# Two decoder blocks on one core: mixers of the first block in another order, and five borders between stages with other waits

## What is computed

```python
def first_block(x, ...):
    h = x
    for i in range(DEPTH):
        z = rms_norm(h, g_mix[i]) @ w_in[i]
        z_a, z_b, z_c = split_cols(z, (A_COLS, B_COLS, C_COLS))
        y_a = chunked_spatial_gating(z_a, ...)
        y_b = rwkv7_time_mix(z_b, ...)
        y_c = nsa_attention(z_c, ...)
        h = h + jnp.concatenate([y_a, y_b, y_c], axis=-1) @ w_out[i]
        hn = rms_norm(h, g_ffn[i])
        f = swiglu(hn, ...) if i % 2 == 0 else moe_swiglu(hn, router_w[j], router_b[j], ...)
        h = h + f
        gate = jax.nn.sigmoid(rms_norm(h, g_ple[i]) @ ple_gate_w[i])
        h = h + (p[i] @ ple_proj_w[i]) * gate
    return rms_norm(h, g_final)

def second_block(x, c, ...):
    for l in range(DEPTH):
        h = rmsnorm(x, norm_mix_g[l]) * (1.0 + sc1) + sh1
        ...
        x = x + g1 * (mix @ w_out[l])
        h = rmsnorm(x, norm_ffn_g[l]) * (1.0 + sc2) + sh2
        x = x + g2 * ((jax.nn.silu(h @ ffn_w1[l]) * (h @ ffn_w3[l])) @ ffn_w2[l])
    return rmsnorm(x, final_g)
```

## Time and profile before

| | |
|---|---|
| median of 3 runs | 2163.87 us (2160.41 to 2163.98) |
| the profiled execution | 2163.64 us, of which the span is 2162.3 us |
| busy share of the span | PE 97%, DVE 34%, ACT 18%, POOL 3% |
| mixers of layer 0 up to the start of its feed-forward part | to 212.4 us |
| the same mixers in layer 1 | 467.64 us later |
| mixture of experts | about 694 to 1396 us |
| borders mixb / ffnb of the second model | 1448 and 1806.6 / 1566 and 1924.7 us |

### The profile page before, as it was taken

The page is one execution under the profiler, slowest core; times in us unless marked ns, Lnnn a source line. Parts: engine busy times, 40 slices in busy tenths (PEclk is TensorE's granted clock), DMA queues, the critical chain, the costliest instruction groups (busy, mean ns, idle before and its releaser), DMA issues.

```text
span 2162.3 us, 28139 instructions
## 1 busy us (share of the span) xinstructions
PE 2092.4 (97%) x11815; PEld 1203.5 (56%) x11815; DVE 726.4 (34%) x1486; ACT 399.0 (18%) x896; POOL 60.7 (3%) x63
## 2 busy tenths in 40 slices
PE   8989999999978899999999999999999999999998
PEld 5665777765754333322333233366677775757775
DVE  2664376322773100000000000137546643831112
ACT  2344000032452000000101001153300002410001
POOL 0021000000110000000000000000000000000000
PEclk9999999999989999999999999999999999999999
DMA  6222985333222999999999999733677642474130
GB/s 233 90 109 87 424 348 219 113 123 117 87 122 102 406 426 416 417 425 413 425 414 425 425 424 425 287 139 122 257 307 267 239 182 83 133 321 144 61 127 20
DMA packets 61235, 535.26 MB, mean 248 GB/s; under 512 B 9200, under 2 KB 9712, under 8 KB 23120
## 3 DMA queue, kind: packets, MB, share of 16 engines
q1 hardware_dynamic: 49216, 474.30, 54.1%
q10 hardware_dynamic: 9216, 50.34, 6.4%
q0 software_dynamic: 2672, 8.78, 1.1%
HBM read 527.74 MB, written 7.75 MB: 248 GB/s over the span
## 4 chain that ended last, share of the span: by engine, by line
PE 85%; DVE 8%; DMA 4%; ACT 2%; issue 1%; POOL 0%; DVEq 0%; SPq 0%; ACTq 0%
PE ps L92 85%; DVE ring L92 5%; DMA ring<-in_moe 4%; DVE stat L92 1%; ACT ring L92 1%; DVE natural L92 0%; DVE gates L92 0%; DVE transposed L92 0%; POOL ring L92 0%; DVE residual L92 0%; ACT natural L92 0%; ACT L92 0%; DMA residual<-in_x 0%; ACT z L92 0%; DVE z L92 0%
## 5 line engine op out<-in xcount | busy, mean ns | idle before, releaser
L92 PE MATMUL ps<-ring 128*32 128x512 f32 (+10 forms) x3784 | 537.4, 521 | 22.0 <-DMA ring<-in_moe 8.4
L92 PE MATMUL ps<-ring,z 128*32 128x512 f32 (+3 forms) x2048 | 476.3, 584 | 5.3 <-ACT ring L92 4.5
L92 PE MATMUL ps<-ring,transposed 128*128 128x384 f32 (+4 forms) x1408 | 470.3, 490 | 3.1 <-DVE transposed L92 2.4
L92 PE MATMUL ps<-transposed,ring 128*128 128x257 f32 (+2 forms) x2128 | 470.4, 379 | 1.3 <-DVE transposed L92 1.3
L92 PEld LDWEIGHTS ps<-transposed,ring 128*128 128x128 f32 (+1 forms) x2128 | 400.2, 189 | 85.3 <-issue 30.4
L92 PEld LDWEIGHTS ps<-ring 128*32 128x32 f32 (+4 forms) x3784 | 200.0, 130 | 302.0 <-issue 279.4
L92 PEld LDWEIGHTS ps<-ring,transposed 128*128 128x128 f32 x1408 | 260.4, 191 | 185.2 <-issue 61.3
L92 PEld LDWEIGHTS ps<-ring,z 128*32 128x32 f32 (+2 forms) x2048 | 172.3, 139 | 254.3 <-issue 240.4
L92 DVE TENSOR_TENSOR z<-z,ps 128x256 f32<-128x256 f32 (+4 forms) x100 | 43.0, 430 | 627.7 <-ACT z L92 607.0
L92 ACT COPY z<-ps 128x256 f32<-128x256 f32 (+6 forms) x110 | 45.7, 415 | 507.7 <-PE ps L92 507.2
L92 ACT ACTIVATE z<-ps 128x256 f32<-128x256 f32 (+2 forms) x87 | 32.6, 374 | 421.8 <-PE ps L92 212.0
(11 more groups left out here) (154 smaller groups left out, 1011.5 us busy)
## 6 DMA issues: line engine op xcount, KB each, us to landing
ring<-in_moe SPq DMA_DIRECT2D x87, 2048.0 KB, 19.3
ring<-in_ffn SPq DMA_DIRECT2D x66, 1536.0 KB, 9.6
ring<-in_moe SPq DMA_DIRECT2D x90, 1024.0 KB, 17.8
ring<-in_w_in SPq DMA_DIRECT2D x25, 1536.0 KB, 6.6
z<-in_ada ACTq DMA_DIRECT2D x48, 768.0 KB, 5.3
ring<-in_w_out SPq DMA_DIRECT2D x12, 1536.0 KB, 6.9
natural<-in_ada ACTq DMA_DIRECT2D x16, 768.0 KB, 5.9
ring<-in_ple_gate SPq DMA_DIRECT2D x4, 1536.0 KB, 8.4
```

Of the source, the lines that this page charges most:

```text
L92: self.ins = None if self.book.counting else op(*args, **kw)
```

## The change

The calls of the mixers of both layers of the first model stand in another order in four places; one copy goes from DVE to ACT; the maximum is written negated at once; and five borders (one in layer 1 of the first model, two ffnb, two mixb) have other waits. The same number of bytes is moved.

```diff
     def act_norm(s, i, ready="{s}.h{i}{e}"):
         for e in range(2):
+            if s[:4] == "ffnb" and (i, e) == (1, 1):
+                act.wait_ge(f"{s}.turned11")
             act_square(s, i, e, HALVES, ready.format(s=s, i=i, e=e))
...
+    def pe_turn_sum(s, i, q, ready):
+        pe.part("turn")
+        for k in range(4):
+            mm(ps[:, turn_bank(s, i, q), k * P:(k + 1) * P], h[:, i, (4 * q + k) * P:(4 * q + k + 1) * P], C("ident"), k == 0, False)
+        pe.then_inc(f"{s}.half{i}{q}")
+        pe.wait_ge(ready)
+        for k in range(4):
+            mm(ps[:, turn_bank(s, i, q), k * P:(k + 1) * P], xn[:, i, (4 * q + k) * P:(4 * q + k + 1) * P], C("ident"), False, k == 3)
+        pe.then_inc(f"{s}.turned{i}{q}")
...
                 add[:, n:n + 1], ALU.mult, ALU.add)
+            if n == 0:
+                dve.then_inc(f"{s}.first{i}")
...
-            if t == 0:
+            if (s[:4], t, i, part) == ("mixb", 0, 1, 0):
+                pe.wait_ge(f"{s}.first{i}")
+            elif t == 0:
                 pe.wait_ge(f"{s}.xt{i}{part}")
             for k in range(4 * part, 4 * part + 4):
+                if (s[:4], t, i, k) == ("mixb", 0, 1, 1):
+                    pe.wait_ge(f"{s}.xt{i}0")
...
-        dve(V.tensor_reduce, mx, at_rows_of(u), AXX, ALU.max)
-        dve(V.tensor_scalar, mx, mx, -1.0, None, ALU.mult).then_inc(f"at.max{l}{u}")
+        dve(V.tensor_reduce, mx, at_rows_of(u), AXX, ALU.max, negate=True).then_inc(f"at.max{l}{u}")
...
-    def dve_rw_hv(l):
+    def act_rw_hv(l):
...
-        pe.wait_ge(f"rw.n{l}")
+        pe.wait_ge(f"rw.n{l}", f"rw.inv{l}51")
...
         pe_rw_xlx(l, 5)
-        pe_at_turn_w(l, 0, f"at.masked{l}1")
         pe_rw_hv(l)
         pe_rw_solve(l)
+        pe_at_turn_w(l, 0, f"at.masked{l}1")
+        pe_rw_inside(l)
         pe_at_scores(l, 2, f"at.pt{l}0")
-        pe_rw_inside(l)
...
         pe_rw_state(l, 1)
+        pe_at_scores(l, 4, f"at.pt{l}2")
         pe_rw_state(l, 2)
-        pe_at_scores(l, 4, f"at.pt{l}2")
...
         pe_at_values(l, 2)
+        pe_at_turn_w(l, 3, f"at.masked{l}4")
         pe_at_cmp_values(l, 0)
-        pe_at_turn_w(l, 3, f"at.masked{l}4")
...
         act_at_compressed(l)
+        act_rw_hv(l)
+        act_at_exp(l, 1)
         act_at_pt(l, 0)
-        act_at_exp(l, 1)
         act_at_pt(l, 1)
+        act_at_exp(l, 2, 0, 2)
+        act_rw_turn_g(l)
+        act_at_exp(l, 2, 1, 2)
         act_at_cmp_exp(l)
-        act_at_exp(l, 2)
-        act_rw_turn_g(l)
...
+        act_at_pt(l, 3)
+        act_rw_norm_root(l)
         act_at_out(l, 0)
-        act_rw_norm_root(l)
-        act_at_pt(l, 3)
...
         dve_at_mask(l, 1)
+        dve_rw_inverse(l, 5)
         dve_at_gate(l, 0)
         dve_at_max(l, 1)
-        dve_rw_inverse(l, 5)
-        dve_rw_hv(l)
         dve_rw_solve(l)
+        dve_at_gate(l, 1)
+        dve_rw_inside(l)
         dve_at_mask(l, 2)
-        dve_at_gate(l, 1)
         dve_at_max(l, 2)
-        dve_rw_inside(l)
         dve_at_cmp_mask(l)
+        dve_at_gate(l, 2)
+        dve_at_mask(l, 3)
+        dve_rw_chunks(l)
         dve_at_cmp_weights(l)
-        dve_at_mask(l, 3)
-        dve_at_gate(l, 2)
-        dve_rw_chunks(l)
         dve_at_max(l, 3)
...
-        if l == 1:
-            dve_router()
         for i in range(NT):
             dve_residual(s, f"ffn{l}", i, banks=BANKS1)
             dve_scale_xt(f"ffn{l}", i, column(l, "g_ffn"))
+            if l == 1 and i == 0:
+                dve_router()
...
-        for q in range(2):
-            pe_turn_plain(f"ffnb{l}", 1, q)
+        pe_turn_plain(f"ffnb{l}", 1, 0)
+        pe_turn_sum(f"ffnb{l}", 1, 1, f"mixb{l}.read11")
...
         dve.part("residual")
+        dve.wait_ge(f"ffnb{l}.half11")
         dve_add_residual(1, 1, xn[:, 1, 512:1024]).then_inc(f"ffnb{l}.h11")
```

More of the change, by code:

```diff
@@ L1247, in pe_rw_hv @@
         pe.then_inc(f"rw.hv{l}")
-    def dve_rw_hv(l):
-        dve.part("rw")
-        dve.wait_ge(f"rw.hv{l}")
-        dve(V.tensor_copy, rw_n4[:, :, :, 0:HD], bank(4, i=NT, e=4)).then_inc(f"rw.n{l}")
+    def act_rw_hv(l):
+        act.part("rw")
+        act.wait_ge(f"rw.hv{l}")
+        act(S.copy, rw_n4[:, :, :, 0:HD], bank(4, i=NT, e=4)).then_inc(f"rw.n{l}")
     def pe_rw_solve(l):
         pe.part("rw")
-        pe.wait_ge(f"rw.n{l}")
+        pe.wait_ge(f"rw.n{l}", f"rw.inv{l}51")
         for g in range(2):
```

## The result

| | before | changed |
|---|---|---|
| median | 2163.93 us (4 runs, 2160.41 to 2164.03) | 2147.68 us (4 runs, 2147.35 to 2149.46) |
| span of the profiled execution | 2162.3 us | 2146.4 us |
| ratio, with its 95% interval | | 0.9931 [0.9919, 0.9944] |

The changed kernel is 16.2 us faster; 19.1 were forecast. The median lies in the range, 2.7 us above the predicted 2145.0. Four stretches give the 15.9 us of the spans. The two layers' mixers gave 3.5 and 4.9 (forecast 5.5 each), the router's place 4.45 (4.4) and 0.65 more in the routing behind it, the mixb borders 0.64 each (0.65), the ffnb borders 0.73 each (1.2). That is 16.2; the expert stretch gave back 0.4.

What follows compares the result with a forecast made beforehand. PE was taken to bound most of the chain, DMA the experts. Mixers 11.0, router 4.4, ffnb 2.4 and mixb 1.3 summed to 19.1 us, taking the kernel to 2145.0 us, range 2142 to 2152.5.

Steps and rivals of the forecast that it cites:

- The two layers' mixers: Reordered mixer calls start the low part of the output product earlier: 5.5 us per layer, 11.0 in all.
- the router's place: Layer 1: the router's DVE instructions move behind the first tile's scaled xt, into a gap; gain 4.4 us, at least 2.3.
- the mixb borders: At two borders one product fits into PE's idle time before the half of xt arrives: 0.65 us each, 1.3 together.
- the ffnb borders: At two borders products of h run in PE's idle time, starting the feed-forward part earlier: 1.2 us each, 2.4 together.
- the expert stretch: Expert weights, DMA-bound behind the routing: the stretch keeps its length and only starts earlier; gain and cost 0 by itself.
- The clock ahead of solve: With hv ahead of PE's wait the clock may stay up, so solve takes 1.8 us instead of 3.54.
- The rival in which the clock falls all the same: PE stays at 1.2 GHz through solve; a layer gains only 2.0 us, total 2151.5 us; chance 0.22.
- From gate of unit 2 to the maximum of unit 4: DVE is the chain here: 21.4 us instead of 18.9, with the maximum out at 172.8.
- the cover: PE's spare time, through at 174.9 and waiting for ACT until 176.0, absorbs about 1 us of low clock.
- the low end of 2.0: Lower bound of a layer's mixer gain in us, worked out for PE staying at 1.2 GHz until 144.6.
- The slower rival: A late hv copy blocks ACT's exps; no layer gain from 142.4, kernel slower from 146.4, 2171 us at 150; chance 0.06.
- The signs that the prediction named: Profile checks: product start about 176, full clock 138 to 144, unit 2's gate 151.4, first expert issue 678.8, shorter border waits.

Runs made afterwards that it cites:

- e5: Changed kernel plus four products of constants, 384 wide and never read, in PE's 3.2 us wait ahead of the second state; 2146.87 us.
- e9: e5 plus one more unread product of 384 columns on each side of turn_w of unit 2; 2145.47 us.
- e1: Changed kernel with all five borders (router, ffnb, mixb) put back, leaving the mixers' change alone; 2155.10 us.
- e4: Changed kernel with the old plain turn at both ffnb borders instead of the sum on PE; 2149.71 us.
- e3: Changed kernel with ACT's root of the time mix's norm moved ahead of pt of unit 3; 2149.58 us.
- e10: Changed kernel without the early first product at the two mixb borders; 2149.20 us.
- e2: Kernel before with only the router's call moved behind the first residual; 2158.97 us.
- e7: Changed kernel with turn_w of unit 0 ahead of hv and solve on PE again; 2159.08 us.
- e8: Changed kernel with the copy of hv back on DVE, ahead of gate of unit 0; 2149.58 us.
- e6: Changed kernel with PE's read and turn of the gated part ahead of the compressed turn, and DVE's compressed weights moved; 2148.53 us.

## Why the prediction was right, and where it was too high

**The clock ahead of solve: right.** hv left PE at 135.47 (forecast 135.4), hidden behind ACT's copies, which end at 136.29, with 0.8 us to spare (0.9 forecast). Its duration was read wrongly: inside has 96 records in the earlier trace rows's trace and not 112, and the 32 of hv took 1.15 us and not 0.9; hv began 0.2 earlier than in the walk, which hides it. PE's wait ahead of solve is 1.55 us, and the clock stayed up: solve 1.96, and 1.00 through inside, in both layers. The rival in which the clock falls all the same at this place did not happen.

**From gate of unit 2 to the maximum of unit 4: the step that failed.** The prediction put 21.4 us here and the end at 172.8; it was 174.87. Of the 2.07, 0.25 is the late gate, 0.24 the second state's round trip (0.79 for the 0.55 that e5 and e9 show at full clock), 1.38 the root (1.65 for 0.27), and 0.2 is spread. The prediction had seen that PE would wait longer ahead of the second state, and put the price of a lower clock at about 1 us, covered by PE's reserve: "If this cover is gone it costs up to 0.5." It reckoned the cover at the end of the stretch, where PE indeed still waits for ACT (0.98). But the delay reaches ACT's queue sooner: the values are late, so is turn_w of unit 3, so is pt, and the root that DVE needs stands behind pt. The prediction said that DVE has "no long wait left between 151 and 173" and named a wait for PE there as a sign of being wrong. There were two: 0.79 us for PE, of which 0.55 was in the old order as well, and the 1.65 for ACT, which it had not looked for.

That the clock is the cause is shown, not only argued. Where the two values groups took 1.0 to 1.2 each, the root's wait was 0.27 (layer 1 of the changed kernel; e5, e9), and where both took 1.8 to 1.9 it was 1.6 and more, in e1 as well. In between the wait follows them one to one: groups of 3.04, 3.34 and 3.75 us together go with waits of 0.91, 1.21 and 1.63 (e4, e1, e1). e9 removes the low clock by products that compute nothing needed, and gets 53.71 and 54.12, near the 53.3 of the forecast. e3 shows that moving the root alone gains nothing. What changed is not that the clock falls in this stretch, for it did in the old order too, but that the values now stand inside the low part of it.

The Trainium skill, in "TensorE: Matmul & The Clock Gate", Part 1, has half rate as the state that an idle array falls back to and that activity lifts. The runs agree: 0.50 behind the 3.20 us wait, 1.00 once the wait is filled. The prediction named this rule as speaking against the change at the second state and for it at solve, and both came true. How long the clock stays low behind equal waits is another matter: 3.20 and 3.19 us gave 1.91 and 1.16 for the compressed values.

**The size of the mixers' term.** Four kernels have the same order of mixers (changed, e1, e4, e10). Their eight layers took 53.95 to 55.33, mean 54.57, against 58.8: a gain of 4.25 per layer for 5.5, far above the low end of 2.0 given for it. Part of this gain is the draw of before's profile: against the 57.96 and 58.10 of e2, where the old order ran solve in 1.96, it is 3.5. That most executions of before lie with its profile (see the last section) is luck for the forecast, which priced solve from this one profile.

**The router: right, and a little short.** 4.45 for 4.4. What was not forecast is the 0.65 that the routing itself gave: its products run 1.7 us faster at full clock, of which a new wait of PE, 0.78 for DVE, takes back a part.

**The experts: nearly right.** Their first issue came 13.56 us earlier, their end (PE at 1387.10 for 1400.30) 13.20 earlier. So the stretch kept its length within 0.4 us and absorbed nothing. The twelve profiles have 705.88 to 707.04 us for it, so that these 0.4 lie inside its spread.

**mixb: right. ffnb: the mechanism right, the term mis-sized.** Four products of `h` were priced "at 0.13 each as before". The earlier trace rows shows transposes, one record each; these are sums in PSUM, real fp32 products of two records, 8 + 8 = 16 records for the eight. From the transposes of the first half to the feed-forward part PE works through 2.24 us without idle time (1549.78 to 1552.02). Before, it was 2.97 us, from the row below to 1566.61: four transposes, the wait of 1.86, four transposes.

```profile
1563.64 0.61 PE L92 MATMUL ps<-constants,residual 128*128 128x128 f32 x4
```

PE itself became the bound, and 1.2 became 0.73. The same text had counted "one product is two records" rightly at mixb.

**The slower rival.** It did not happen, as hv had its 0.8 us to spare. Its mechanism is real. In e7 layer 0 began 1.19 us earlier than before, so that the copy's end at 141.04 stands at 142.2 in the times of the earlier trace rows, just ahead of the 142.4 from which the prediction had a layer gain nothing. The layers were 2.4 and 0.6 us longer than before. The price per microsecond was about right (in layer 1 the copy ended 5.0 us later than in the changed kernel, and the layer is 4.9 longer than the mean of its order), but it is taken from a gain of 4.25 and not of 5.5, and in layer 0 the low clock through solve (3.68 us) comes on top, which the threshold left out. e8 shows the other side: on DVE the copy costs 0.9 us per layer.

**The signs that the prediction named.** PE's product behind ACT's copy started at 178.01 and not at 176, and the first expert issue came at 680.62 and not at 678.8: both are the shortfall of the mixers. The clock, the gate of unit 2, the ffnb wait (0) and the mixb wait (0.30) came as named. One sign was worked out wrongly: it has layer 1's scaled `xt` 467.6 us behind layer 0's, which takes off the router's part of the 472.09 but not layer 1's own gain in the mixers. By its own terms that was 462.1; measured were 670.72 - 208.06 = 462.66.

## What to carry to other kernels

Where a reordering makes one of PE's waits longer, price the low clock behind it and follow it into the queue of the next engine, not only to the end of the stretch; a few products that nobody reads, placed in the wait, can keep the clock (e9, 2.2 us), but in e5, layer 1, they failed where the clock had fallen in an earlier wait. Count records, not products: a transpose is one, an fp32 product two. When the same order is profiled several times, compare its stages between the profiles; their spread shows which stage has two outcomes.

## What the runs showed of the hardware that was not expected

- The same instructions behind the same wait come out at either clock. Layer 0 and layer 1 of the changed kernel have waits of 3.20 and 3.19 us, and the values behind them took 1.91 and 1.16. In the old order, solve took 3.54 in both layers of before and 1.96 in both of e2. One profile is one draw of this, worth 0.8 us per layer in the old order and up to 1.4 in the new one.
- The shorter wait ahead of solve (1.51 to 1.55 us, once 0.87) left solve at 1.96 us in all sixteen profiled layers of the eight kernels that have this order. The waits of 2.90 (before and e2, turn_w 1.45 to 1.97 for 1.09), 3.20 (changed) and 3.27 (e7, turn_w 1.97) were followed by the low clock in both layers each; what differs is how soon it came back. Of the two waits of 2.15 and 2.17 in e6, the clock fell in the first and not in the second.
- The executions of before fall into two groups. Of the 34 in the rounds of the experiments, 9 have a mean granted clock of 0.989 or 0.990 and took 2159.25 to 2161.55 us, 25 have 0.986 to 0.988 and took 2163.05 to 2167.93. Its profile (0.988) is of the larger group. Solve alone does not explain it: in two layers it is worth 1.6 us, and the groups' middles lie 3 us apart. What the rest is stays open.
- With the clock kept, DVE's and ACT's chain sets the end of the stretch: PE's idle time ahead of the low part grew from 0.98 to 1.24 us in e5 and e9, so that, by this reading and tried by no run, more speed on PE alone would bring nothing there.
